# Moved bias products, later first jobs of a sparse attention, earlier scalings, and two tiles of the last norm summed by TensorE

## The reference

```python
def conformer_conv(h, ...):
    u = h @ w_pw1 + b_pw1;  a, gate = split(u);  u = a * sigmoid(gate)
    u = depthwise_conv(u, w_dw) + b_dw            # width 31, causal
    return silu(layernorm(u, ln_g, ln_b)) @ w_pw2 + b_pw2

def dilated_attention(...):                        # uses rel_bias, one table of buckets for all heads

def second_block(x, ...):
    hn = rms_norm(h, mix_norm_pre);  proj = hn @ w_in
    # retention on 8 heads, and a sparse attention on 8 heads: an indexer scores the keys,
    # the best 128 of each query are kept, then softmax attention with one key and value head
    mixed = concatenate([ret_out, att_out]) @ w_out
    h = h + rms_norm(mixed, mix_norm_post)
    up = causal_dwconv(rms_norm(h, ffn_norm_pre) @ w_up);  g, u = split(up)
    return h + rms_norm((silu(g) * u) @ w_down, ffn_norm_post)
```

## Time and profile before

| | |
|---|---|
| median of 3 runs | 1819.21 us (1819.13 to 1819.86) |
| the profiled execution's own time | 1819.52 us |
| its span, first to last instruction | 1817.7 us |
| busy: PE, DVE, ACT, POOL | 97%, 57%, 39%, 9% |
| mean granted TensorE clock | 0.989 of 2.4 GHz |

### The profile page before, as it was taken

How to read it: one execution, slowest core, us unless ns; L and a number is a source line. 1 busy time by engine, 2 the same in 40 slices (tenths; PEclk the granted TensorE clock), 3 DMA queues, 4 the chain that set the end, 5 groups by cost and what they waited for, 6 DMA issues and landing times.

```text
span 1817.7 us, 21121 instructions
## 1 busy us (share of the span) xinstructions
PE 1765.9 (97%) x8106; PEld 1404.2 (77%) x8106; DVE 1029.6 (57%) x1287; ACT 707.8 (39%) x1095; POOL 172.1 (9%) x128
## 2 busy tenths in 40 slices
PE   7999799999999999999999999989999899999997
PEld 6887588888888878778888888756557778888886
DVE  6998664433444555654424444559856677537753
ACT  5655532212233344332212323465564444324431
POOL 0010010000000100110000004471200200000001
PEclk9999999999999999999999999999999999999998
DMA  5210322322232311132312231523112122322221
GB/s 181 70 47 28 99 94 101 115 95 83 102 118 78 124 70 53 65 105 103 127 70 93 92 127 70 153 73 116 50 62 70 70 93 101 119 70 92 101 96 47
DMA packets 28052, 164.63 MB, mean 91 GB/s; under 512 B 4511, under 2 KB 5675, under 8 KB 11596
## 3 DMA queue, kind: packets, MB, share of 16 engines
q1 hardware_dynamic: 25088, 158.11, 24.7%
q10 hardware_dynamic: 2892, 5.55, 1.0%
HBM read 156.28 MB, written 4.47 MB: 88 GB/s over the span
## 4 chain that ended last, share of the span: by engine, by line
PE 88%; DVE 8%; ACT 2%; issue 1%; POOL 1%; DMA 0%; DVEq 0%; SPq 0%; ACTq 0%; POOLq 0%
PE PS L620 26%; PE PS L622 26%; PE PS L621 26%; PE PS L726 1%; PE PS L727 1%; PE PS L725 1%; DVE W_lo L1821 1%; DVE WK L2266 1%; DVE SSUM L2307 1%; DVE TOP L2264 1%; PE PS L1045 1%; ACT W_hi L1154 1%; POOL ISC L1765 1%; PE PS L1056 1%; DVE PS L2443 0%
## 5 line engine op out<-in xcount | busy, mean ns | idle before, releaser
L620 PE MATMUL PS<-H_hi,W_hi 128*128 128x512 f32 x1600 | 641.6, 401 | 18.3 <-DVE H_lo L1801 14.0
L622 PE MATMUL PS<-H_hi,W_lo 128*128 128x512 f32 x1600 | 626.1, 391 | 0.0
L621 PE MATMUL PS<-H_lo,W_hi 128*128 128x512 f32 x1600 | 625.6, 391 | 0.0
L1154 ACT ACTIVATE W_hi<-W_raw 128x2048 fp32r<-128x2048 f32 (+2 forms) x130 | 262.6, 2020 | 674.2 <-PE PS L622 674.2
L620 PEld LDWEIGHTS PS<-H_hi,W_hi 128*128 128x128 f32 x1600 | 301.9, 189 | 105.1 <-issue 41.2
L1821 DVE TENSOR_TENSOR W_lo<-W_raw,W_hi 128x2048 fp32r<-128x2048 f32 (+2 forms) x130 | 331.2, 2548 | 59.5 <-ACT W_hi L1154 59.1
L622 PEld LDWEIGHTS PS<-H_hi,W_lo 128*128 128x128 f32 x1600 | 301.5, 188 | 64.6
L621 PEld LDWEIGHTS PS<-H_lo,W_hi 128*128 128x128 f32 x1600 | 302.2, 189 | 59.5 <-issue 1.2
L620 PE MATMUL PS<-HID_hi,W_hi 128*128 128x512 f32 x640 | 250.3, 391 | 7.5 <-DVE HID_lo L1962 7.4
L622 PE MATMUL PS<-HID_hi,W_lo 128*128 128x512 f32 x640 | 249.7, 390 | 0.0
L621 PE MATMUL PS<-HID_lo,W_hi 128*128 128x512 f32 x640 | 249.7, 390 | 0.0
(11 more groups left out here) (289 smaller groups left out, 1522.0 us busy)
## 6 DMA issues: line engine op xcount, KB each, us to landing
W_raw<-in_inp SPq DMA_DIRECT2D x13, 1024.0 KB, 4.8
W_raw<-in_pw SPq DMA_DIRECT2D x11, 1024.0 KB, 4.8
W_raw<-in_gu0a SPq DMA_DIRECT2D x11, 1024.0 KB, 4.8
W_raw<-in_gu0b SPq DMA_DIRECT2D x11, 1024.0 KB, 4.8
W_raw<-in_gu1a SPq DMA_DIRECT2D x11, 1024.0 KB, 4.8
W_raw<-in_gu1b SPq DMA_DIRECT2D x11, 1024.0 KB, 4.8
W_raw<-in_gu2a SPq DMA_DIRECT2D x11, 1024.0 KB, 4.8
W_raw<-in_gu2b SPq DMA_DIRECT2D x11, 1024.0 KB, 4.8
```

The source lines that it names most:

```text
L620: nc.tensor.matmul(dst[:], wh, x_hi[:, k, :], start=(k == first), stop=False)
L621: nc.tensor.matmul(dst[:], wh, x_lo[:, k, :], start=False, stop=False)
L622: return nc.tensor.matmul(dst[:], wl, x_hi[:, k, :], start=False, stop=(k == last))
L1154: nc.scalar.activation(W_hi[b][:, 0:n], W_raw[b][:, 0:n], ACT.Copy).then_inc(w_hi, 1)
```

## The change

1. `bias_products` goes from ahead of the layer norm's sums to behind its last square sum, into banks 2 to 4 instead of 1 to 3; on ACT the three copies and the transfer go from ahead of the squares to behind the square root and the load of the SiLU table.
2. The jobs of the sparse attention start at slots 94, 99, 104, 109, and then at 116 + 7n, instead of 84 + 7q.
3. After `wout`, the last two `final_scaled` run ahead of the last unit's copies, no longer inside `add_normed`.
4. In the last norm, DVE makes the scaled tiles 4 and 5 first, into SBUF (`T4`). PE sums X and the scaled tile into a bank with two products by the identity, and ACT copies the bank to X. DVE adds only tiles 0 to 3. The orders of the output are 0, 4, 2, 6 on SP and 5, 1, 3, 7 on ACT, the latter behind both bank copies. The semaphores `conv_pe` and `conv_pe_taken` are renamed and used for this too.

```diff
+PE_LAST = [4, 5]
-DSA_AT, DSA_STRIDE = 84, 7
+DSA_STARTS = [94, 99, 104, 109] + [116 + 7 * n for n in range(13)]
+DSA_SLOT = {s + r: (n, r) for n, s in enumerate(DSA_STARTS) for r in range(5)}
...
-            for m in (0, 2, 6, 4):
+            for m in (0, 4, 2, 6):
                 if m >= DT - POOL_LAST:
                     sp.wait_ge(x_pool, m - DT + POOL_LAST + 1)
+                elif m in PE_LAST:
+                    sp.wait_ge(bank_taken, len(TAKE_AT) + PE_LAST.index(m) + 1)
...
-                    nc.tensor.matmul(PS[1 + g][0:GROUP_HEADS, 0:DIAG], ...
+                    nc.tensor.matmul(PS[2 + g][0:GROUP_HEADS, 0:DIAG], ...
...
-            bias_products()
             pe.wait_ge(ln_sum, 7)
             nc.tensor.matmul(PS[0][:], ones, SSUM[:], start=True, stop=False)
             pe.wait_ge(conv_made, 6)
             nc.tensor.matmul(PS[0][:], ones, CV[:, 7, :], start=False, stop=True).then_inc(ln_sum_ready, 1)
-            pe.wait_ge(fvec_made, 3)
             for n, m in enumerate(LN_SUMS):
...
+            bias_products()
+            pe.wait_ge(fvec_made, 3)
             linear("pw2", HID_hi, HID_lo, ready=after(ln_lo_made, 0))
...
-                q, r = divmod(g - DSA_AT, DSA_STRIDE)
+                q, r = DSA_SLOT.get(g, (-1, -1))
...
             token_spread(AUX[2], r_ps)
+            for n, m in enumerate(PE_LAST):
+                nc.tensor.matmul(PS[n][:], ident, X[:, m, :], start=True, stop=False)
+            for n in range(len(PE_LAST)):
+                pe.wait_ge(f_applied, 8 + n + 1)
+                nc.tensor.matmul(PS[n][:], ident, T4[n][:], start=False, stop=True).then_inc(bank_summed, 1)
...
-            for g in range(3):
-                take_bias(g)
-            act.wait_ge(fvec_made, 3)
-            act.dma_start(bias_rows...
             warm_table(ACT.Sqrt)
...
             warm_table(ACT.Silu)
+            for g in range(3):
+                take_bias(g)
+            act.wait_ge(fvec_made, 3)
+            act.dma_start(bias_rows...
...
-            for m in (1, 5, 3, 7):
+            for n, m in enumerate(PE_LAST):
+                act.wait_ge(bank_summed, len(PE_TAPS) + n + 1)
+                nc.scalar.activation(X[:, m, :], PS[n][:], ACT.Copy).then_inc(bank_taken, 1)
+            act.wait_ge(bank_taken, len(TAKE_AT) + len(PE_LAST))
+            for m in (5, 1, 3, 7):
...
                     u = j.plus(L.base)
+                    if name == "wout" and j.c == L.n - 1:
+                        final_normed(j.c)
                     for half in range(2):
...
                 if split:
-                    final_scaled(DT - 2)
                     last_lo(0)
...
                 if split:
-                    final_scaled(DT - 1)
                     last_lo(1)
...
-                for m in range(tiles):
+                if k:
+                    for i, m in enumerate(PE_LAST):
+                        nc.vector.scalar_tensor_tensor(out=T4[i][:], in0=Y[:, m, :], scalar=vec(gain, m), in1=AUX[1][:],
+                                                       op0=ALU.mult, op1=ALU.mult).then_inc(f_applied, 1)
+                ahead = len(PE_LAST) if k else 0
+                for m in range(tiles - ahead):
```

More of the change, by code:

```diff
@@ L496, in build @@
         diag_made = sem("diag_made")
-        conv_pe = sem("conv_pe")
-        conv_pe_taken = sem("conv_pe_taken")
+        bank_summed = sem("bank_summed")
+        bank_taken = sem("bank_taken")
         fg_made = sem("fg_made")
@@ L707, in bias_products @@
                 for g in range(3):
-                    nc.tensor.matmul(PS[1 + g][0:GROUP_HEADS, 0:DIAG], table[:, GROUP_HEADS * g:GROUP_HEADS * (g + 1)],
+                    nc.tensor.matmul(PS[2 + g][0:GROUP_HEADS, 0:DIAG], table[:, GROUP_HEADS * g:GROUP_HEADS * (g + 1)],
                                      onehot[:, g, :], start=True, stop=True).then_inc(fvec_ps, 1)
@@ L726, in conv_tap @@
                 nc.tensor.matmul(AUX[p][:], d_hi, x_lo, start=False, stop=False)
-                nc.tensor.matmul(AUX[p][:], d_lo, x_hi, start=False, stop=t == CONV_WIDTH - 1).then_inc(conv_pe, 1)
+                nc.tensor.matmul(AUX[p][:], d_lo, x_hi, start=False, stop=t == CONV_WIDTH - 1).then_inc(bank_summed, 1)
             L = layers["pw1"]
@@ L1243, in take_conv @@
             def take_conv(p):
-                act.wait_ge(conv_pe, PE_ENDS[p])
+                act.wait_ge(bank_summed, PE_ENDS[p])
                 m = PE_TILES[p][0]
-                nc.scalar.activation(CV[:, m, :], AUX[p][:], ACT.Identity, bias=vec("b_dw", m)).then_inc(conv_pe_taken, 1)
+                nc.scalar.activation(CV[:, m, :], AUX[p][:], ACT.Identity, bias=vec("b_dw", m)).then_inc(bank_taken, 1)
             def conv_hi(p):
@@ L1253, in conv_hi @@
                 if p >= 2:
-                    act.wait_ge(conv_pe, PE_ENDS[p - 2])
+                    act.wait_ge(bank_summed, PE_ENDS[p - 2])
                 n = SEQ + CONV_WIDTH - 1
@@ L1262, in diagonals @@
                 if c >= 3:
-                    act.wait_ge(conv_pe, CHUNK * (c - 2))
+                    act.wait_ge(bank_summed, CHUNK * (c - 2))
                 for x, (m, t) in enumerate(PE_TAPS[CHUNK * c:CHUNK * (c + 1)]):
@@ L1297, in take_bias @@
                 act.wait_ge(fvec_ps, g + 1)
-                nc.scalar.activation(fvec[:, g, :], PS[1 + g][0:GROUP_HEADS, 0:DIAG], ACT.Copy).then_inc(fvec_made, 1)
+                nc.scalar.activation(fvec[:, g, :], PS[2 + g][0:GROUP_HEADS, 0:DIAG], ACT.Copy).then_inc(fvec_made, 1)
             for g in range(SLOTS, SLOTS * L.n):
@@ L1309, in _ @@
             split_hi(act, L, At(L.n - 1))
-            for g in range(3):
-                take_bias(g)
-            act.wait_ge(fvec_made, 3)
-            act.dma_start(bias_rows.rearrange("(g h) d -> h g d", h=GROUP_HEADS), fvec[:]).then_inc(rows_out, 16)
             warm_table(ACT.Sqrt)
@@ L1323, in _ @@
             warm_table(ACT.Silu)
+            for g in range(3):
+                take_bias(g)
+            act.wait_ge(fvec_made, 3)
+            act.dma_start(bias_rows.rearrange("(g h) d -> h g d", h=GROUP_HEADS), fvec[:]).then_inc(rows_out, 16)
             for m in range(DT):
@@ L1673, in _ @@
             nc.scalar.activation(R[:], AUX[2][:], ACT.Copy).then_inc(r_copied, 1)
-            for m in (1, 5, 3, 7):
-                if m >= DT - POOL_LAST:
+            for n, m in enumerate(PE_LAST):
[3 more added lines that the diff above has]
+            for m in (5, 1, 3, 7):
+                if m in PE_LAST:
+                    pass
+                elif m >= DT - POOL_LAST:
                     act.wait_ge(x_pool, m - DT + POOL_LAST + 1)
@@ L1704, in _ @@
             pool.wait_ge(stat_ready, 1)
-            for n, (m, made, count) in enumerate([(0, conv_made, 1), (1, conv_pe_taken, 1), (2, conv_made, 2), (3, conv_pe_taken, 2),
+            for n, (m, made, count) in enumerate([(0, conv_made, 1), (1, bank_taken, 1), (2, conv_made, 2), (3, bank_taken, 2),
                                                   (4, conv_made, 3), (6, conv_made, 4), (5, conv_made, 5)]):
@@ L1887, in conv_joined @@
                 m = PE_TILES[p][0]
-                dve.wait_ge(conv_pe, PE_ENDS[p])
+                dve.wait_ge(bank_summed, PE_ENDS[p])
                 nc.vector.tensor_tensor(CV[:, m, :], CV[:, m, :], AUX[p][:], ALU.add).then_inc(conv_made, 1)
@@ L2444, in add_normed @@
                                                    op0=ALU.mult, op1=ALU.mult).then_inc(f_applied, 1)
-                    dve.wait_ge(f_applied, 8 * k + m + 1)
+                    dve.wait_ge(f_applied, 8 * k + ahead + m + 1)
                     nc.vector.tensor_tensor(X[:, m, :], X[:, m, :], t[:], ALU.add).then_inc(x_ready, 1)
```

## The result

The changed kernel takes 1828.34 us (median of 5, 1827.92 to 1832.55), the kernel before 1819.21: a ratio of 1.0054, 95% interval 1.004 to 1.0069. It is slower, and outside the range. The profiled execution is the slowest of the five: 1832.55, with a span of 1830.8 and a mean granted clock of 0.987, where the other four show 0.990. A clock lower by 0.003 over 1830 us is 5.5 us of work (an estimate), about the 4.2 between this execution and the median.

The account below looks back on a forecast made before the run. TensorE was taken to be busy nearly throughout, so only its waits or hideable work could give gains. Parts 1 to 4 summed as -2.0 + 2.5 - 0.45 - 1.1 = -1.05, giving 1818.2 us, range 1812.8 to 1822.8.

Parts of the forecast that it names:

- the job work owed: At slot 100 of `inp`: PE still owes three quarters of a job of 2.5 us, 1.9 us.
- the meeting at 147: Slot 147 of `inp`: job 8's exponentials stand on ACT ahead of `ret_take`, so PE waits at slot 148, +3.0 us.
- the division at 150: Slot 150 of `inp`: no reciprocal right behind DVE's division any more, -4.3 us; a third of the earlier gain lost, +1.
- the meeting at 162: Slot 162 of `inp`: ACT's exponentials and scaling stand ahead of `ret_take`, with DVE idle, +1.7 us.
- the meeting at 189: Slot 189 of `inp`: the same meeting as at slot 162, with DVE idle, +1.7 us.
- the last jobs: End of `inp`: nothing ahead of `ret_take` at slot 201, -0.8 us; last values at slot 204, nearer the end, +0.5.
- The second count: Part 2 in `inp`, by following both queues: +2.7 us to slot 164 and +3.9 at the end.
- rival B: Slots 147, 162, 189: waits before `ret_take` drop the clock, about 1.5 us three times; part 2 +7.5, total 1823.2; chance 0.13.
- It then waits 7 us at slot 99: Slot 99 of `inp`: DVE's backlog holds PE 7 us, instead of 5.2 at slot 91, and the clock falls again.
- The low clock behind it: Behind slot 100 of `inp`: half of 4 to 5 us is lost at low clock, +2.3 us, bounds 1 and 3.
- its -0.45: After `wout`: DVE reaches the norm 0.7 us earlier but the spread of 1/rms limits it, -0.45, between 0 and -0.5.
- The four transfers of ACT follow at the old pace (1.32 us for three): End of the last norm: the last of ACT's transfers starts at 1813.6, before at 1814.7, so -1.1 us.

Follow-up runs that it names:

- the slots alone: The kernel before with part 2 alone, the attention jobs at slots 94, 99, 104, 109 and 116 + 7n: 1833.41 on 1819.79, ratio 1.0079.
- ACT's order changed: The kernel before with the change's slots, and on ACT the squares and copy of the retention heads ahead of the jobs' steps: 1825.9, ratio 1.0032.
- with DVE's: The kernel before with the change's slots, and on DVE a job's maximum and reciprocal ahead of the split of the weights: 1826.48, ratio 1.0034.
- the bias alone: The kernel before with part 1 alone, the bias products, their copies and the transfer moved: 1818.05 on 1819.76, ratio 0.9988.
- all but the slots: The changed kernel with the jobs back at slots 84 + 7q, so parts 1, 3 and 4 alone: 1817.98, ratio 0.9991.
- part 2 alone, slots from 88: The kernel before with the attention jobs at slots 88 + 7q, all 7 slots apart: 1827.17, ratio 1.004.
- the version with all parts: The changed kernel with jobs 7 slots apart from slot 88 and, on ACT, the retention heads' squares and copy first: 1815.53 on 1819.76, ratio 0.9977.
- part 4 alone: The kernel before with the last part of the change alone, tiles 4 and 5 summed by TensorE: 1819.71 on 1819.97, ratio 0.9999.
- the version with the early transfer: The version with all parts, with ACT issuing the transfer of output tile 1 ahead of its two bank copies: 1814.55, ratio 0.9972.

## Why the prediction was wrong

**Part 2 failed.** I expected +2.5; alone it is +13.6. My terms by stage, beside what the slots alone did to the delay (-0.8 at slot 91, which is the execution's own; the job work owed, 1.9, is put where it is paid, in the last jobs):

| from slot to slot | terms | delay in us | measured |
|---|---|---|---|
| 91 to 146 | -1.6 + 2.3 + 0.5 = +1.2 | -0.8 to 2.2 | +2.9 |
| 146 to 150, the meeting at 147 | +3.0 | to 8.1 | +6.0 |
| 150 to 159, the division at 150 | -4.3 + 1.0 = -3.3 | to 4.9 | -3.2 |
| 159 to 165, the meeting at 162 | +1.7 | to 7.3 | +2.3 |
| 165 to 191, the meeting at 189 | +1.7 | to 8.8 | +1.5 |
| 191 to 207, the last jobs | +1.9 - 0.8 + 0.5 = +1.6 | to 10.1 | +1.3 |
| 207 to 214, start of `wout` | 0 | to 12.4 | +2.2 |
| sum | +5.9 | | +13.1 |

Three steps failed.

- *"I take +2.5, under both, because nearly every term is an upper one."* No row supported that. The terms summed to +5.9, and no measured stage lies more than 0.3 below its term. The second count, +2.7 at slot 164 and +3.9 at the end, was further off: by the same profile it is +8.1 at slot 165 and +10.9 at slot 207. With +5.9 in place of +2.5 the total is 1821.6.
- *"split, maximum (1.0), exponentials (1.1), squares and copy (1.1), less the two products that PE still has ... +3.0."* These terms don't give 3.0. With the split of 2.3 to 3.4 us that the same step names they give 5.5 to 6.6, less 1.4 for two products: 4.1 to 5.2. Measured: 4.76, where the kernel before waited 0.5; the other 1.7 of the +6.0 is the low clock behind it, which I had put into rival B alone. With this wait and the undiscounted sum the total is 1822.7 to 1823.8 without the clock, at and above the 1822.8 from which I call it slower. Rival B was the mechanism, at a chance of 0.13. It priced a fall of the clock behind all three waits; the clock fell behind the longest alone, and is 1.00 in the stretches behind those of 1.6 and 1.7 us.
- *"It then waits 7 us at slot 99."* It waits 8.9, 8.8 with the slots alone. My list of DVE's backlog left out the mask added to the next block of the indexer's scores (L2263, 1.24 us), and its split took 2.77, not 2.2. The low clock behind it, put at 2.3 with bounds 1 and 3, lies at the upper bound: from slot 100 to 104 the delay grows by 2.9 us.

That the first stall would only move, the gain at the division, and the meetings at 162 and 189 were right. That the order of the steps within a slot is the cause was shown by changing it alone: with ACT's order changed, the loss of the slots falls from 13.6 to 5.9 us, with DVE's to 6.5. Both shorten the same chain at slot 147, DVE's the stall at slot 99 too, and together they leave a change that is no slower. Of the last +2.2, 0.9 is a longer wait for the first split of `wout` (2.4 us, before 1.5), in every kernel whose last job lies four slots later. 1.3 is a low clock in the products behind it: in seven of the nine profiles with the longer wait, in none of the five with the shorter. Why two were spared stays open.

**Part 1**: right. -2.0 predicted, -2.28 at `pw2`, -1.7 in the time of the bias alone. PE's wait ahead of `pw2` shrank to 5.37, near the 5.3 forecast, and the clock fell in it all the same.

**Part 3**: its -0.45 is there where the clock is as before. With all but the slots, the last copy starts at 1421.60 and the first use at 1426.10: 4.50 in place of 4.94 us. In the changed kernel the clock fell ahead of the spread, and it is 5.65. With a low clock the spread ends last, and then the part gains nothing: 5.42 us without the part (part 2 alone, slots from 88), 5.43 with it (the version with all parts). The spread ran wholly or partly at the low clock in 10 of the 14 profiles, so the gain hung on a clock that I took for granted.

**Part 4**: -1.1 predicted, +0.5 in the changed kernel. The clock was nearly as forecast: it rose at 1822, 4.0 us behind DVE's first step, where the sum has 3.6 (1809), and ACT's last copy ended at 1824.98, 6.97 behind that step, where the sum has 6.85 (1812.25). The step that failed is *"The four transfers of ACT follow at the old pace (1.32 us for three)"*. Four in a row take 2.91 us to issue, and the last starts 9.2 us behind DVE's first step, not 8.2; before it was 9.3. From its start to the end of the span it is 3.6 us, before 3.0. These two, 1.0 and 0.6, are the whole difference. An earlier clock would have helped: with all but the slots it had risen before the passes over X, and the same code took 1812.5 - 1801.15 = 11.35 us, -0.95. That execution is the fastest of its kernel, so this was luck. With part 4 alone, without such a clock, it took +0.3. The Trainium skill (DMA: Bandwidth & Descriptors, "Anatomy of one DMA") gives a transfer issued by GpSimd a fixed 2 us or so, most of it the write receipt of the target memory. These are issued by ACT: 2.1 to 2.2 us when spread out, 3.4 when bunched, and no run here tells how much of either is the receipt.

## What to carry to other kernels

When work is moved along a hand-written order, the price lies less in the work than in what its new slot puts it in front of: list, for each engine's queue, what stands behind the moved step in the same slot, and who waits for it. A step with a late input belongs behind one whose input is ready; two such reorderings were worth nearly as much here as going back to the old slots (9.8 of 10.4 us). And when the terms of a sum are each read from rows, the sum stands: discount one only with a row that shows the overlap. Transfers that are put in a row behind one event need the pace of such a row, not that of spread ones.

## What the runs showed of the hardware

- After the stall of 4.76 us, the granted clock stayed at full through the wait (1.00 from 1290 to 1292) and fell when PE was back at work (0.74, then 0.50). In longer waits it fell inside: at slot 99 it is 0.92 from 1223 to 1225 and 0.50 from 1225, with PE back at 1228.72; ahead of `pw2` it is 0.50 from 192 to 196, with PE back at 195.17. Either way the price is paid by the work behind the wait.
- The length of a wait alone didn't decide. The clock stayed at full behind waits of 1.6 and 1.7 us in the changed kernel, but in the kernel before it is 0.50 from 1302 to 1304, behind two waits of 1.38 and 1.48 us less than 3 us apart.
- The same split of 128x2048 took 2.77 and 2.75 us at slots 98 and 146, and 3.37 in the kernel before, each time beside GpSimd's products. At 1210.94 it took 2.29 beside two of GpSimd's, and there these took 4.67 us, where one alone takes 1.3. So beside each other one or both get longer. The Trainium skill (GPSIMD Engine Reference, "Specifications") says that GpSimd shares its SBUF interfaces with VectorE, with contention when an instruction of VectorE has two inputs in SBUF; the split has, and the rows agree.
- The same four 128x512 passes of the identity over X took 3.16 us in the changed kernel and 2.17 in the version with the early transfer: the clock came back later in the first. Executions of one kernel differed by up to 5.5 us (1814.29 to 1819.84 with all but the slots).
